# The gate stage's units in another order, weights prepared three units ahead

## What is computed

```python
mod = (silu(c) @ w_ada + b_ada).reshape(nb, 6, 1, D_MODEL)          # conditioning, 12288 columns
h = rms_norm(x, norm_g[0]) * (1 + mod[:, 1]) + mod[:, 0]
q, k, v, p, gb, gc, hc, gl = split(h @ w_in, SPLITS)                # gl: 3 gates of 2048
br_c = combine_groups(attention of 3 groups) @ w_attn_br            # samples: keys and values from a cache
br_a = (group_linear(pooled(p)) * pool_scale) @ w_pool_br           # 4 pooling windows
br_b = (gb * causal_dwconv(gc * hc, conv_w)) @ w_conv_br
gates = sigmoid(gl.reshape(nb, t, 3, D_MODEL))
merged = gates[0] * br_a + gates[1] * br_b + gates[2] * br_c
x = x + mod[:, 2] * rms_norm(merged @ w_o, norm_g[1])
h2 = rms_norm(x, norm_g[2]) * (1 + mod[:, 4]) + mod[:, 3]
f = ffn(h2)                                                         # w_up, conv over 3 rows, gelu, w_down
x = x + mod[:, 5] * rms_norm(f, norm_g[3])
```

## Time and profile before

| | us |
|---|---|
| median of 3 runs | 3360.1 (3356.27 to 3360.92) |
| span of the profiled execution, first to last instruction (the profile gives no other time of it) | 3358.2 |
| PE busy | 3202.9 (95%) |
| DVE busy | 1530.5 (46%) |
| ACT busy | 1052.4 (31%) |
| POOL busy | 112.8 (3%) |
| mean rate of all DMA | 120 GB/s |
| granted TensorE clock, mean | 0.975 |

### The profile page before, as it was taken

The page is one execution under the profiler, slowest core; times in us unless marked ns, Lnnn a source line. Parts: engine busy times, 40 slices in busy tenths (PEclk is TensorE's granted clock), DMA queues, the critical chain, the costliest instruction groups (busy, mean ns, idle before and its releaser), DMA issues.

```text
span 3358.2 us, 62863 instructions
## 1 busy us (share of the span) xinstructions
PE 3202.9 (95%) x25170; PEld 3034.8 (90%) x25170; DVE 1530.5 (46%) x2291; ACT 1052.4 (31%) x1474; POOL 112.8 (3%) x211
## 2 busy tenths in 40 slices
PE   5799999989999999999989999999999999999998
PEld 2389998868999999999979999999999999999997
DVE  4742344464444444444365444444443444444445
ACT  4632222223333333333243232322323222232223
POOL 1001001010000000000000000000000000000000
PEclk7899999999999999999999999999999999999998
DMA  7764323244555555554322333233332323323233
GB/s 250 224 198 124 115 79 111 63 125 134 161 164 152 163 163 153 163 163 155 92 88 76 96 96 89 84 95 90 89 92 88 95 84 101 90 79 99 83 95 127
DMA packets 521716, 402.17 MB, mean 120 GB/s; under 512 B 15910, under 2 KB 462570, under 8 KB 520692
## 3 DMA queue, kind: packets, MB, share of 16 engines
q1 hardware_dynamic: 509298, 356.77, 35.6%
q0 software_dynamic: 12240, 42.65, 3.6%
HBM read 383.65 MB, written 20.24 MB: 120 GB/s over the span
## 4 chain that ended last, share of the span: by engine, by line
PE 90%; DVE 4%; issue 2%; DMA 2%; ACT 1%; DVEq 0%; ACTq 0%; SPq 0%
PE X L1348 12%; PE X L1349 12%; PE X L1350 12%; PE Y L1348 11%; PE Y L1349 11%; PE Y L1350 10%; PE BA L1384 4%; DMA raw<-in_w_ada 1%; PE BA L1348 1%; PE BT L1350 1%; PE BO L1350 1%; PE BA L1350 1%; PE BA L1349 1%; PE BT L1349 1%; PE BS L1348 1%
## 5 line engine op out<-in xcount | busy, mean ns | idle before, releaser
L797 DVE TENSOR_TENSOR wlo<-raw,whi 128x1024 fp32r<-128x1024 f32 x684 | 818.3, 1220 | 701.6 <-ACT whi L542 692.3
L1348 PE MATMUL X<-hH,whi 128*128 128x260 f32 x3232 | 932.6, 289 | 31.0 <-issue 15.8
L542 ACT CAST whi<-raw 128x1024 fp32r<-128x1024 f32 x684 | 692.6, 1050 | 848.1 <-PE X L1350 304.8
L1349 PE MATMUL X<-hL,whi 128*128 128x260 f32 x3232 | 921.3, 285 | 0.0
L1350 PE MATMUL X<-hH,wlo 128*128 128x260 f32 x3232 | 920.1, 285 | 0.0
L1348 PE MATMUL Y<-hH,whi 128*128 128x260 f32 x2720 | 772.3, 284 | 0.0
L1349 PE MATMUL Y<-hL,whi 128*128 128x260 f32 x2720 | 768.7, 283 | 0.0
L1350 PE MATMUL Y<-hH,wlo 128*128 128x260 f32 x2720 | 767.8, 282 | 0.0
L1348 PEld LDWEIGHTS X<-hH,whi 128*128 128x128 f32 x3232 | 616.8, 191 | 47.4 <-issue 27.5
L1349 PEld LDWEIGHTS X<-hL,whi 128*128 128x128 f32 x3232 | 617.1, 191 | 1.9
L1350 PEld LDWEIGHTS X<-hH,wlo 128*128 128x128 f32 x3232 | 617.3, 191 | 0.0
(11 more groups left out here) (394 smaller groups left out, 3919.8 us busy)
## 6 DMA issues: line engine op xcount, KB each, us to landing
raw<-in_w_ada SPq DMA_DIRECT2D x192, 512.0 KB, 4.3
raw<-in_w_up SPq DMA_DIRECT2D x176, 512.0 KB, 4.0
raw<-in_w_in SPq DMA_DIRECT2D x164, 512.0 KB, 3.9
raw<-in_w_down SPq DMA_DIRECT2D x88, 512.0 KB, 3.5
raw<-in_w_o SPq DMA_DIRECT2D x32, 512.0 KB, 4.2
k_s<-in_cache_kv_w POOLq DMA_DIRECT2D x48, 128.0 KB, 3.9
d_x<-xT POOLq DMA_DIRECT2D x1, 4160.0 KB, 14.6
xR<-d_x POOLq DMA_DIRECT2D x1, 4160.0 KB, 15.2
```

The lines of the kernel that those rows point to most:

```text
L542: nc.scalar.copy(whi[u.spl], raw[:, u.raw, :]).then_inc(w_hi, 1)
L797: dve.tensor_tensor(wlo[u.spl], raw[:, u.raw, :], whi[u.spl], ALU.subtract).then_inc(w_lo, 1)
L1348: pe.matmul(ps, h, xh, start=first, stop=False)
L1349: pe.matmul(ps, h, xl, start=False, stop=False)
```

## The change

The positions of a turn's units become gate 0, 1, 2, 5, 8, 9; conditioning 3, 4, 6, 7, 10, 11, 13, 14; branch unit 12; convolution unit 15. Before, conditioning units stood at 1, 3, 5, 6, 8, 10, 12, 14, two of the three gate chunks were cut by one and one by two. Now the first and third chunk are whole and conditioning units come in pairs. Each engine's program follows. `lead` gets an argument `ahead`, 3 unless given: the gate stage from its second turn, w_o and the FFN prepare unit l + 3; the stages before and the first gate turn keep 2, and the first turn ends with one further preparation. Where the last 8 units are prepared, `if l < 6` becomes `if l < 5`. The split and raw buffers stay as they are.

In the first turn the tails' copies (`pool_tails`) come after position 0, the last gathers share position 8 with group 0, the groups and poolings come one position earlier, and so does the branch split.

The bias of the 16 tiles of the gate stage no longer comes as a 19th row by a POOL load for each tile. One load at the start (`rowsB`, 64 x 128) is transposed by PE with the other parameters and copied to `bias_cols`; DVE adds it where it copied before. The parameter rows now lie ahead of `xr` in memory, and ACT waits for the store of the attention bias (`bias_st`) before the projections.

Of the diff, most calls of `lead` that only gain the argument 2, the two `l < 5`, the layout of the regions and blank lines are left out.

```diff
@@ -58,7 +58,7 @@
-M_GATE, M_ADA, M_BR, M_CONV = (0, 2, 4, 7, 9, 11), (1, 3, 5, 6, 8, 10, 12, 14), 13, 15
+M_GATE, M_ADA, M_BR, M_CONV = (0, 1, 2, 5, 8, 9), (3, 4, 6, 7, 10, 11, 13, 14), 12, 15
@@ -166,7 +166,8 @@
-    mod_rows = place("mod_rows", [19, 512])
+    mod_rows = place("mod_rows", [P, 512])
+    bias_cols = place("bias_cols", [P, 64])
...
@@ -327,7 +330,7 @@
-            for l in range(13):
+            for l in range(M_BR):
@@ -339,7 +342,8 @@
-            ada_unit(Unit(U_M, 16, it, 14), it + 8, 7)
+            for l in range(M_BR + 1, M_CONV):
+                ada_unit(Unit(U_M, 16, it, l), it + 8, M_ADA.index(l))
@@ -387,6 +391,7 @@
+        gp.dma_start(rowsB, a["b_ada"][0, 4096:].rearrange("(k p) -> k p", p=P)).then_inc(row_in, 16)
@@ -478,9 +483,6 @@
-        with gp.Fori(0, KD) as it:
-            gp.wait_ge(mod_tr, it + 9)
-            mod_bias_row(it + 8)
@@ -534,26 +536,26 @@
-        def lead(base, per, it, l):
-            hi(Unit(base, per, it, l + 2))
+        def lead(base, per, it, l, ahead=3):
+            hi(Unit(base, per, it, l + ahead))
-                    lead(U_ADA, 8, it, l)
+                    lead(U_ADA, 8, it, l, 2)
@@ -589,10 +591,11 @@
+        act.wait_ge(bias_st, 16)
-                    lead(U_QKV + 12 * part, 4, it, l)
+                    lead(U_QKV + 12 * part, 4, it, l, 2)
...
@@ -651,10 +654,11 @@
+            ahead = 2 if isinstance(it, int) else 3
-                if l + 2 == M_BR:
+                if l + ahead == M_BR:
-                lead(U_M, 16, it, l)
+                lead(U_M, 16, it, l, ahead)
@@ -670,8 +674,9 @@
-        gates(0, {0: sample_exp, 12: branch_hi})
+        gates(0, {0: sample_exp, 11: branch_hi})
+        lead(U_M, 16, 0, 15)
...
@@ -796,8 +801,8 @@
-        def lead(base, per, it, l):
-            lo(Unit(base, per, it, l + 2))
+        def lead(base, per, it, l, ahead=3):
+            lo(Unit(base, per, it, l + ahead))
...
@@ -849,6 +854,7 @@
+        dve.tensor_copy(bias_cols, Y[:, 0, 80:144]).then_inc(par_out, 1)
...
@@ -1033,6 +1039,7 @@
+        def pool_tails():
@@ -1107,8 +1115,8 @@
                     if n == 2:
-                        lead(U_M, 16, it, 14)
-                        lead(U_M, 16, it, 15)
+                        for l in range(M_BR + 1, 16):
+                            lead(U_M, 16, it, l, ahead)
@@ -1123,14 +1131,18 @@
                     dve.wait_ge(br_out, it * 3 + (n + 2))
-            mod_columns(dve, it + 8, it + 9)
+            dve.wait_ge(mod_tr, it + 10)
+            bias = bias_cols[:, bass.ds(it * 4, 4)].unsqueeze(2).to_broadcast([P, 4, 9])
+            dve.tensor_tensor(mods[:, bass.ds(it * 4 + 32, 4), :], BT[:, 0:36].rearrange("p (k n) -> p k n", n=9), bias,
+                              ALU.add).then_inc(mod_out, 1)
         sample_scores()
-        gates(0, {1: [sample_probs], 2: [probs_columns, lambda: pool(0)], 3: [lambda: sample_outputs(0)],
+        gates(0, {0: [pool_tails], 1: [sample_probs], 2: [probs_columns, lambda: pool(0)], 3: [lambda: sample_outputs(0)],
                   4: [lambda: sample_outputs(2), lambda: pool(1)], 6: [lambda: sample_outputs(4)],
-                  7: [lambda: sample_outputs(6), lambda: pool(2)], 8: [sample_columns], 9: [lambda: group(0)],
-                  10: [lambda: group(1), lambda: pool(3)], 11: [lambda: group(2)], 12: [lambda: group(3), branch_lo]})
+                  7: [lambda: sample_outputs(6), lambda: pool(2)], 8: [sample_columns, lambda: group(0)],
+                  9: [lambda: group(1), lambda: pool(3)], 10: [lambda: group(2)], 11: [lambda: group(3), branch_lo]})
+        lead(U_M, 16, 0, 15)
...
@@ -1385,13 +1397,21 @@
+        def turn_pieces(n):
+            pe.wait_ge(mod_row, n + 2)
+            pe.wait_ge(mod_out, n + 1)
+            for i in range(4):
+                m = pe.matmul(BT[:, 9 * i:9 * i + 9], mod_rows[0:18, i * P:(i + 1) * P], sel[0:18, :], start=True, stop=True)
+            m.then_inc(mod_tr, 1)
-                m = pe.matmul(BT[:, 9 * i:9 * i + 9], mod_rows[:, i * P:(i + 1) * P], sel, start=True, stop=True)
+                m = pe.matmul(BT[:, 9 * i:9 * i + 9], mod_rows[0:19, i * P:(i + 1) * P], sel, start=True, stop=True)
@@ -1422,8 +1442,9 @@
-        pe.wait_ge(row_in, 16 * 6)
+        pe.wait_ge(row_in, 16 * 7)
+        pe.transpose(Y[:, 0, 80:144], rowsB, ident[0:64, 0:64])
@@ -1433,7 +1454,7 @@
-        pe.wait_ge(par_out, 4)
+        pe.wait_ge(par_out, 5)
@@ -1594,30 +1615,36 @@
-            chunk(U_M, 16, it, M_GATE[0], X, x_free, it * 3 + C_M, between=lambda: mods(0), apart=2)
+            def behind_gate(i):
+                return lambda: behind(M_GATE[i])
+            chunk(U_M, 16, it, M_GATE[0], X, x_free, it * 3 + C_M, between=behind_gate(0))
             behind(M_GATE[1])
-            mods(1)
-            chunk(U_M, 16, it, M_GATE[2], Y, y_free, it * 3 + C_M, between=lambda: (behind(M_GATE[2]), mods(2), mods(3)), apart=3)
+            chunk(U_M, 16, it, M_GATE[2], Y, y_free, it * 3 + C_M, between=lambda: (behind(M_GATE[2]), mods(0), mods(1)), apart=3)
             behind(M_GATE[3])
+            mods(2)
+            mods(3)
+            chunk(U_M, 16, it, M_GATE[4], X, x_free, it * 3 + (C_M + 1), between=behind_gate(4))
+            behind(M_GATE[5])
             mods(4)
-            chunk(U_M, 16, it, M_GATE[4], X, x_free, it * 3 + (C_M + 1), between=lambda: (behind(M_GATE[4]), mods(5)), apart=2)
-            behind(M_GATE[5])
-            mods(6)
+            mods(5)
             branch(u, X, x_free, it * 3 + (C_M + 2), 4, 4, 2).then_inc(w_used, 1)
+            behind(M_BR)
+            mods(6)
             branch(u, Y, y_free, it * 3 + (C_M + 2), 0, 6, 4).then_inc(w_used, 1)
-            turn_mods(it + 8)
+            turn_pieces(it + 8)
         sample_scores()
-        gates(0, {2: probs_columns, 3: lambda: (pe.wait_ge(ptail_out, 2), sample_values(0)), 4: lambda: sample_values(2),
-                  6: lambda: sample_values(4), 7: lambda: sample_values(6), 8: last_gathers, 9: lambda: group(0),
-                  10: lambda: group(1), 11: lambda: group(2), 12: lambda: group(3)})
+        gates(0, {1: lambda: pe.wait_ge(ptail_out, 2), 2: probs_columns, 3: lambda: sample_values(0), 4: lambda: sample_values(2),
+                  6: lambda: sample_values(4), 7: lambda: sample_values(6), 8: lambda: (last_gathers(), group(0)),
+                  9: lambda: group(1), 10: lambda: group(2), 11: lambda: group(3)})
```

More of the change, by code:

```diff
@@ L177, in layer @@
     assert e <= L0
-    (xr, rb, rows1, rowsF, rowsC, rowsP, relb, onehot, brows, ssq, rs, diag, xT), end0 = region(
+    (rowsB, rows1, rowsF, rowsC, rowsP), _ = region(
+        L0, ("rowsB", [64, P], F32), ("rows1", [80, P], F32), ("rowsF", [88, 3, P], F32), ("rowsC", [16, CC], F32),
+        ("rowsP", [120, PW], F32))
+    (xr, rb, relb, onehot, brows, ssq, rs, diag, xT), end0 = region(
         L0, ("xr", [P, KD, T], F32), ("rb", [P, T], F32),
-        ("rows1", [80, P], F32), ("rowsF", [88, 3, P], F32), ("rowsC", [16, CC], F32), ("rowsP", [120, PW], F32),
         ("relb", [33, 12], F32), ("onehot_s", [33, G, BW], F32), ("brows", [HG, G, BW], F32),
@@ L536, in scalar_program, with hi @@
     def scalar_program(act):
-        def hi(u, first=False):
+        def hi(u, start=False):
             act.wait_ge(w_raw[u.raw], u.arrived)
-            if not first:
+            if not start:
                 act.wait_ge(w_used, u.spl_free)
             nc.scalar.copy(whi[u.spl], raw[:, u.raw, :]).then_inc(w_hi, 1)
-        def lead(base, per, it, l):
-            hi(Unit(base, per, it, l + 2))
+        def lead(base, per, it, l, ahead=3):
+            hi(Unit(base, per, it, l + ahead))
         act.wait_ge(c_in, 48)
@@ L550, in scalar_program @@
         for l in range(2):
-            hi(Unit(0, 0, 0, l), first=True)
+            hi(Unit(0, 0, 0, l), start=True)
         def tiles(part):
@@ L613, in scalar_program @@
                                      accum_out=ls[:, h:h + 1]).then_inc(s_exp, 1)
-                lead(U_PC, 16, it, 2 * c)
+                lead(U_PC, 16, it, 2 * c, 2)
                 act.wait_ge(p_tr, m + 1)
@@ L622, in scalar_program @@
                 ins.then_inc(p_out, 1)
-                lead(U_PC, 16, it, 2 * c + 1)
+                lead(U_PC, 16, it, 2 * c + 1, 2)
                 pair = PAIR[c % 2]
@@ L757, in scalar_program @@
         for l in range(9):
-            if l < 6:
+            if l < 5:
                 lead(U_END, 8, 0, l)
```

## The result

The changed kernel takes 3390.4 us (median of 4 runs, 3389.29 to 3393.47), the kernel before beside it 3359.8. The ratio is 1.0092, with a 95% interval of 1.0078 to 1.0107: slower by about 30 us, where 9 were forecast and the range ended at 3376. The profiled execution has a span of 3387.7 us, 29.5 more than before, at a mean granted clock of 0.968 (0.975 before).

A forecast was written before the change was run, and what follows sets the result against it. PE was taken as fully busy in steady gate turns, leaving only the first turn, seams and loop ends. Start 0.4, first turn 6.2, clock 2.0, seam 0.4 gave +9.0 us: 3369.1, range 3359 to 3376.

The forecast's parts named there:

- Steady turns, 0: Fifteen steady gate turns: PE stays fully busy, the third unit prepared ahead is covered by PE's work; 0 us.
- First gate turn, the waits, +6.2: First gate turn: new order delays the branch unit by 3.4 us and the stretch behind it by 2.8; +6.2 us.
- The k_s waits: First gate turn: PE waits about 3.4 us for values of samples 2 and 3, 2.7 for 6 and 7.
- the working's +2.8: First gate turn, branch unit's start to convolution unit: 13.3 us instead of 10.6, entered as +2.8 us.
- The clock in the first turn, +2.0 (0 to +8): First gate turn: PE's clock falls behind one of the new waits; +2.0 us, range 0 to +8.
- I take one fall: First gate turn: one clock fall at 2.0 us assumed, since two of three earlier rows fell.
- 3 to 6 us: First gate turn: assumed time at clock 0.5 after a fall, half of it lost, 1.5 to 2.7 us.
- Rival 2: First gate turn: clock falls at all three new waits, +4 to +6 us more, 3374; chance 0.15.
- w_o and FFN, 0: w_o and FFN stages: preparing weights three units ahead changes nothing; 0 us, far bound 14.
- The nine pieces themselves: FFN loop's turns back: PE's nine idle pieces, 15.8 us in all, taken as unchanged, 0; far bound 14.
- rival 4: FFN loop's ends: the load beside each lengthens the wait, half the far bound, +7 us, 3376; chance 0.07.
- Start and seam: Start: extra copy and transpose, +0.4 us. Gate stage to w_o: third preparation delays the product, +0.4 us.

The follow-up runs named there:

- the kernel before with its two mends: Kernel before with PE's ten FFN turns written out and first-gate-turn branch operands' low parts awaited one by one; 3337.3 us (0.9927), again 3337.1 (0.9925).

## Why the prediction was wrong

**Steady turns, 0: right, for a reason it gave only in part.** They even gained 0.09 each. That the third unit ahead "has the time of units n to n+2" holds; what it would cost to leave it out, 62 us, was not asked.

**First gate turn, the waits, +6.2: right.** From the start of the turn to the first value pair 20.27 us (forecast 20.4). The k_s waits were 2.15 and 3.83, in sum 6.0 (3.4 and 2.7, 6.1). From gate unit 9's end to the branch unit 20.1 (19.5), from there to the convolution unit 13.1 (13.3; the working's +2.8 for this stretch should read 2.7).

**The clock in the first turn, +2.0 (0 to +8): the term that was mis-sized.** 15.9 less 6.2 is 9.7. By stretches: the second pair behind its wait took 5.5 us instead of 3.85 (+1.7), the fourth 7.15 (+3.3), gate unit 8 7.2 instead of the 5.9 of other gate units (+1.3), the convolution unit and the small products 6.75 instead of 4.1 (+2.6), in sum 8.9. "I take one fall" failed: there were three, and the longest cost 4.6 us by itself. Taking "3 to 6 us" at the low clock was also short: it lasted 10. Rival 2 had the mechanism, with 8 us in all at most. Its argument against, that the clock had stayed up behind a wait of 2.39, was one row that decided nothing; behind 2.48 at 780.18 it was down. What decides it at one of these waits stays open; a longer wait at the same place is what the runs show beside it (2.26 against 1.49, 2.21 against 1.53). In five kernels with this order, alike up to there but for one pooling's place, it took 66.9 to 71.0 us from the turn's start to behind gate unit 9, so this term has a spread of 4 us of its own.

**w_o and FFN, 0: the step that failed.** "The nine pieces themselves are nearest ... and I take 0" was a choice between 0 and 14, and the stage took 14.3 more. The load beside the wait was the mechanism: rival 4. It said that the load "may be through"; in fact the code packet meets it: about 350 KB of the load's 512 moved in the microsecond around the usual time of that packet, at each of the nine ends. The waits alone grew by 4.0, inside the bound. The 10.3 us of the clock behind them (six more falls at 1.5, and 1.2 in one turn) stood in no case. It could have: the nine turns of the kernel before already had two lengths, 139.8 and 141.3, and the difference was the price.

**Combining.** Rivals 2 and 4 were priced as if only one could come. Each is slower than the forecast, they lie in different stages and nothing excludes one by the other. Together they give 9 + 5 + 7 = 21 us, 3381, above the range's end of 3376, and with the 10 us of the clock in the FFN about the measured 30.

**Start and seam.** The first gate unit came 1.1 earlier, not 0.4 later; it varies by 7 us between executions, so this can't be told. The seam was +0.2 (0.4). w_o and norms took 1.6 more: about 1.0 is a longer low clock at w_o's start (2.7 against 1.7 us lost). That w_o stretch also shows in the kernel before with its two mends, whose steady turns are the old ones (230.5), and not in the old order with three ahead (228.6); its cause stays open.

## What to carry to other kernels

A loop with a long body can pay a code fetch at every branch back. Here PE's FFN body, about 2400 matmuls and weight loads, paid it each time; the gate stage's, about 800, and w_o's, about 400, never did. A transfer of yours that runs at that moment lengthens it, so ask where each load lies against the loop's end, or write the turns out on the engine that bounds. Price a new wait twice: once for its length, and once for the matmuls behind it that may run at 1.2 GHz. The second can be the larger part (10 us against 4 in this FFN, 9 against 6 in the first turn). Rivals in different stages can come together, and the range has to hold their sum.

## What the runs showed of the hardware

- The fetch at PE's branch back shows in the DMA view as 16 KB packets of kind "instruction". From the start of the first packet to PE's next matmul it is 2.6 to 3.1 us at 66 of 67 loop ends of eight kernels, and 3.5 at one. That is the packet's own time, 0.9 to 1.8 us, and then 1.6 to 1.8 us at all 67: PE's wait follows the packet's end. The wait is 1.6 to 1.8 us on average in kernels with no load in full flow there, 2.2 to 2.3 beside a 512 KB load.
- PE's last matmul mostly starts 0.9 to 1.0 us after an undisturbed packet is seen, and a load in flight moves the packet by up to 1 us.
- Of the 67 waits, the 22 below 1.8 us were never followed by a fall of the clock; of the 45 from 1.8 to 2.9 us, 31 were, and at 2.50 and 2.76 it stayed up. In the first gate turn, where PE's work is sparser, it also fell behind waits of 1.5 and 1.7.
- The fully written-out FFN moves fewer instruction packets over the whole kernel, not more:

```profile
q8 instruction: 142, 2.33, 0.3%
```

  against 158 in the kernels with the loop, and no wait of PE for code shows in its turns.
- While PE stood still before the fourth pair the clock was not down yet: in the 4.8 us before 724.8, in which it stood for 3.8, 0.99 was granted, and the 10 us of work behind it got 0.50. So a wait's own window doesn't show what it costs.
